# Where the Strassen pairs stand in a down projection: six in place of five in its second half, and the first half's one tile pair later

## The reference

```python
x = x + (jax.nn.silu(u_gate) * u_val) @ w_down[i]     # (256 x 5504) @ (5504 x 2048)
```

## Time and profile before

| | us |
|---|---|
| median of 3 runs | 1431.72 (1431.7 to 1431.96) |
| profiled execution, time | 1431.3 |
| its span, first to last instruction | 1429.5 |

### The profile page before, as it was taken

One profiled execution on the slowest core, in us unless ns is written; L12 is line 12 of the kernel. 1 busy time (PEld: TensorE's weight loads), 2 busy tenths in 40 slices (PEclk: granted clock), 3 DMA queues, 4 the chain that ended last, 5 costly groups with the idle time before them and its releaser, 6 DMA issues.

```text
span 1429.5 us, 19805 instructions
## 1 busy us (share of the span) xinstructions
PE 1419.2 (99%) x7085; PEld 1205.2 (84%) x7085; DVE 1046.8 (73%) x1304; ACT 778.7 (54%) x944; POOL 172.8 (12%) x116
## 2 busy tenths in 40 slices
PE   9999999999999999999999999999999999999997
PEld 7888888888888888888888888888888888888886
DVE  7576777868687865566777767777777988887755
ACT  7555655545454544455555555555555555555644
POOL 0044144110000000000111101111011110000000
PEclk9999999999999999999999999999999999999999
DMA  9655555454655665465656566565665555556653
GB/s 326 197 176 162 162 173 167 149 188 163 222 193 188 220 237 193 155 212 179 193 174 205 178 191 194 173 203 182 191 196 177 205 195 197 171 203 209 232 201 120
DMA packets 190876, 273.47 MB, mean 191 GB/s; under 512 B 11744, under 2 KB 103136, under 8 KB 190688
## 3 DMA queue, kind: packets, MB, share of 16 engines
q1 hardware_dynamic: 190384, 272.30, 58.1%
q10 hardware_dynamic: 432, 0.37, 0.1%
HBM read 270.53 MB, written 2.10 MB: 191 GB/s over the span
## 4 chain that ended last, share of the span: by engine, by line
PE 98%; DVE 1%; issue 0%; DMA 0%; ACT 0%; ACTq 0%; POOLq 0%; POOL 0%; DVEq 0%
PE aux L853 11%; PE main L853 11%; PE main L674 10%; PE main L675 10%; PE main L676 10%; PE aux L862 6%; PE main L862 6%; PE main L732 5%; PE main L733 5%; PE main L734 5%; PE aux L732 3%; PE aux L733 3%; PE aux L734 3%; PE aux L675 2%; PE aux L676 2%; PE aux L674 2%
## 5 line engine op out<-in xcount | busy, mean ns | idle before, releaser
L1439 DVE TENSOR_TENSOR w_lo<-raw,w_hi 128x1024 fp32r<-128x1024 f32 (+1 forms) x481 | 593.0, 1245 | 319.3 <-ACT w_hi L1133 318.6
L1133 ACT ACTIVATE w_hi<-raw 128x1024 fp32r<-128x1024 f32 (+1 forms) x481 | 505.3, 1052 | 502.7 <-PE main L676 155.2
L674 PE MATMUL main<-w_hi,xT 128*128 128x512 f32 x510 | 201.4, 395 | 0.3 <-DVE w_lo L1908 0.3
L675 PE MATMUL main<-w_lo,xT 128*128 128x512 f32 x510 | 198.6, 389 | 0.0
L676 PE MATMUL main<-w_hi,xT 128*128 128x512 f32 x510 | 198.5, 389 | 0.0
L853 PE MATMUL aux<-xT,w_hi 128*128 128x512 f32 x704 | 169.8, 391 | 0.0
L853 PE MATMUL main<-xT,w_hi 128*128 128x512 f32 x672 | 163.0, 391 | 0.0
L853 PEld LDWEIGHTS aux<-xT,w_hi 128*128 128x128 f32 x704 | 129.3, 188 | 25.3 <-issue 0.3
L853 PEld LDWEIGHTS main<-xT,w_hi 128*128 128x128 f32 x672 | 123.2, 188 | 23.6
L2033 POOL TENSOR_TENSOR act<-cv 128x512 f32<-128x512 f32 (+1 forms) x22 | 71.9, 3268 | 418.8 <-DVE cv L1663 418.8
L674 PEld LDWEIGHTS main<-w_hi,xT 128*128 128x128 f32 x510 | 95.8, 188 | 20.0 <-DVE xT L1466 1.0
(11 more groups left out here) (319 smaller groups left out, 2159.3 us busy)
## 6 DMA issues: line engine op xcount, KB each, us to landing
raw<-in_w_up SPq DMA_DIRECT2D x336, 256.0 KB
raw<-in_w_in SPq DMA_DIRECT2D x136, 512.0 KB
raw<-in_w_down SPq DMA_DIRECT2D x84, 512.0 KB
raw<-in_w_out SPq DMA_DIRECT2D x32, 512.0 KB
raw<-in_w_ple_gate SPq DMA_DIRECT2D x32, 512.0 KB
raw<-in_w_branch_a SPq DMA_DIRECT2D x16, 512.0 KB
raw<-in_w_branch_b SPq DMA_DIRECT2D x16, 512.0 KB
raw<-in_w_in SPq DMA_DIRECT2D x15, 256.0 KB, 5.8
```

Source lines behind the costliest of these rows:

```text
L674: pe.matmul(acc, th, wh, start=first, stop=False)
L675: pe.matmul(acc, th, wl, start=False, stop=False)
L1133: ac.activation(w_hi[:, u % RING, :, 0:w], raw[:, u % RING, :, 0:w], ACT.Copy).then_inc(hi_full, 1)
L1439: dve.tensor_tensor(w_lo[:, u % RING, :, 0:w], raw[:, u % RING, :, 0:w], w_hi[:, u % RING, :, 0:w].bitcast(F32), ALU.subtract).then_inc(lo ...
```

## The change

One line: where the Strassen pairs stand.

```diff
-SEVEN_AT = ((5, 8, 11, 14, 17), (5, 8, 11, 14, 17))
+SEVEN_AT = ((6, 9, 12, 15, 18), (4, 7, 10, 12, 15, 17))
```

## The result

The changed kernel takes 1435.66 us (median of 10 runs, 1435.07 to 1436.11) against 1431.71 in the same comparison: a ratio of 1.0026, 95% interval 1.0018 to 1.0035. The prediction was 1435.0, range 1432.4 to 1436.6. The profiled execution took 1435.64, its span is 1433.8 and its granted clock 0.999.

The account below looks back on a forecast made before the run. PE, busy 98%, was taken to bound the kernel, with DVE nearly the bound in the down projection. PE waits of 4.4 plus 0.4 between the pairs, minus 0.68, 0.55 and 0.25, gave +3.3 us: 1435.0, range 1432.4 to 1436.6.

Parts of the forecast that it names:

- One Strassen pair more: Down projection, PE: one more pair of units takes 21 matmuls in place of 24, minus 0.68 us.
- First pair later: First pair of chunks one tile pair later: PE's waits for activation sums and a weight's low part go, minus 0.55 and 0.25.
- Turn: Between the pairs of chunks: ACT's copy waits for later products, delaying DVE's additions; PE loses 0.4 us, bounds 0 and 0.8.
- In hand at the second pair's first: DVE's lead over PE at the second pair's first Strassen pair: 0.3 us, 0.15 after hand-over, bounds 0 and 1.23.
- Rounds: Second pair, L1688 to next L1688: 15.97 us at distance 3, 12.5 and 11.4 at distance 2; 4.4 of PE waits.
- DVE did not catch up at the turn: Rival, between the pairs: DVE catches up, 1.23 in hand, one join in idle time; +0.8 us, 1432.5, chance 0.20.
- the loads did not land sooner: Rival, loads between L1688 and ACT's split: short rounds' loads land sooner; -1.1 us, 1430.6, chance 0.06.
- All of it worse: Rival, down projection: 0.44 lost a round, nothing in hand, 0.8 between the pairs, 0.5 wait kept; +5.1, 1436.8, chance 0.12.

Follow-up runs that it names:

- the version with one short distance: Changed kernel with second pair at 4, 7, 10, 13, 16, 18, GpSimd's join behind the weight sums, its small activation sums later: 1431.51 us, 1.0000 to before.
- half loads: Changed kernel, but each load of the second pair of chunks brings one row tile of two, 256 KB: 1432.23 us, 1.0005 to before.
- half join: Changed kernel, but the second pair's GpSimd joins, from the second on, add one row tile of two: 1432.39 us, 1.0005 to before.
- later join: Changed kernel, but GpSimd's join waits until the weight sums of the Strassen pair before have ended: 1431.47 us, 1.0000 to before.

## Why the prediction was right

Forecast +3.3 from the rows, measured +3.95 in the medians and +3.8 in the stage. Rows of the changed kernel for steps 2 and 3, PE at units 32 and 38, ACT's copy and DVE's fifth addition:

```profile
1173.25 0.39 PE L734 MATMUL main<-w_hi,a_sums_lo 128*128 128x512 f32 x1
1173.71 0.47 PE L732 MATMUL main<-w_hi,aT_hi 128*128 128x512 f32 x1
...
1189.25 0.39 PE L734 MATMUL main<-w_hi,a_sums_lo 128*128 128x512 f32 x1
1189.82 0.47 PE L732 MATMUL main<-w_hi,aT_hi 128*128 128x512 f32 x1 [0.18 <-DVE w_lo L1439]
```

```profile
1198.27 0.60 ACT L1326 ACTIVATE w_sums<-aux 128x512 f32<-128x512 f32 x1 [2.87 <-PE main L734]
```

```profile
1205.65 0.68 DVE L1756 TENSOR_TENSOR w_sums<-aux,w_sums 128x512 f32<-128x512 f32 x1
```

By its steps:

1. **One Strassen pair more, -0.68.** As said. The stage of the version with one short distance, where PE waits for almost nothing, is 1.28 shorter than before: 0.68 and the two waits of the earlier trace rows (0.8), less the turn's 0.3, make 1.2.

2. **First pair later: -0.55 and -0.25.** The first is right: PE has no gap at the first Strassen pair, and the split behind the first sums is 1.37 ahead of PE. The second is not. PE waits 0.24 at unit 32 and 0.34 at unit 38, 0.8 with restarts, where I took none. The mis-sized term is the round: 16.17, 15.99, 16.22 and 16.10, mean 16.12, so 0.48 lost a round and not 0.32; what was in hand went 1.37, 0.84, 0.49 and was gone at the fourth. I had named this end (0.44 a round, 0.5 stays) and not taken it. In the four other runs that leave the first pair and its joins as in the change, the gaps and restarts here come to 0.3 to 0.6, so the 0.8 is that of one execution.

3. **Turn, +0.4.** 0.17 and a restart of 0.14. The copy starts at 1198.27 behind PE, [2.87 <-PE main L734], 4.6 later than in the earlier trace rows, and the fifth addition ends at 1206.33, 0.06 ahead of PE's start. With the first pair left as it was the turn has no gap, so it is the later last Strassen pair that makes it.

4. **In hand at the second pair's first, 0.3.** It was 0.70, hand-over included: the turn had eaten half of the 1.38, not all.

5. **Rounds.** Long ones 16.01, 16.10 and 15.94 for 15.96; short ones 12.70 and 11.41 for 12.5 and 11.4; the load 4.36 in the short round, so nothing lands sooner there, as taken. The half split takes 1.78 because the join falls beside it, as forecast. The second pair's waits with restarts are 4.3 for 4.4: the 0.4 more in hand at the start went into long rounds that were up to 0.14, and a short one that was 0.2, longer. That the total agrees to 0.1 is luck: these are two misses of about 0.4 that cancel.

So the second pair's waits stood in the rows of before, in their cause and, with that luck, in their total. Their places are only partly as forecast: without restarts nothing is lost behind tile pair 7, 0.73 behind 10, 1.63 behind 12, 0.72 behind 15 and 0.33 behind 17, where I had 0.1 to 0.3 behind 7 and 10, about 2 behind 12 and about 1 behind 17. The 0.5 that is missing from the sum in the stage is the first pair's 0.8, less the 0.2 by which the turn and the second pair came out better, to within 0.1. Of the rivals, DVE did not catch up at the turn (0.70 in hand, not 1.23, and no join of the short rounds fell into idle time), and the loads did not land sooner. The half loads show how far this rival's mechanism is right: with loads shorter by 1.5 the second pair's waits are 1.5 us and not 4.3, since the long rounds fall under 15.64. For the short rounds it is wrong: it takes the load's saving off them whole, which would give 11.0 and 9.9, and they came out at 13.37 and 11.42. The prediction calls the load the largest piece of the round and overlooks that DVE's own work, 11.66 and 10.57, is longer than PE's 10.20 by itself. "All of it worse" was right in one of its parts, the first pair's.

## What to carry to other kernels

Where one engine is at 98% and another feeds it in rounds, compare the round, release to release, with the fed engine's work for the same piece. While the round is shorter, an edit that lengthens it is free; once it is longer, each tenth comes out of what is in hand, and then out of the time. Half a microsecond a round decided some 3 us here. An added piece of work that saves 0.68 cost far more than it saved, because it made two rounds in which PE has 10.20 us of work and VectorE, which feeds it, 11.66 and 10.57. So compare the feeding engine's own busy time with the fed engine's work too: where it is longer, no faster load helps in that round, only what was gained in others. Look first for what lies in the round and needn't: moving one GpSimd instruction behind the release was worth as much as the whole change had lost.

## What the runs showed of the hardware

A VectorE instruction of the kind shown here (TENSOR_TENSOR, both inputs in SBUF) that starts during GpSimd's join stands until shortly before the join's row ends, and then takes its plain time. In the changed kernel the half split that starts at 1270.71 stands until 1271.80 (1.09 over its 0.69), and the join's row ends at 1271.95. With the half join the rows above give 1257.58 and 1257.71, with the later join 1259.67 and 1259.81. So what is lost is what is left of the join when the VectorE instruction starts, less 0.13 to 0.15: 1.1, 0.55 and 0.68 us in these three.

The join stands in the same way. It shows 1.30 where VectorE is idle at its start (1258.51, join later). At 1269.74 in the changed kernel an L1713 that runs until 1270.80 was there first, and the join's row is 2.21 long. So a long GpSimd row can be one that was held itself. The Trainium skill's page "SBUF — State Buffer" (SBUF: two separate sides) says that of two such instructions the one that starts first has the pair of ports which the engines share for the whole instruction, and the other blocks fully. The trace agrees, in both directions.

A load of 512 KB takes 4.1 to 4.4 us from release to use in the changed kernel's second pair, at either distance, and one of 256 KB 2.7: 1.5 us for 256 KB more, with two more loads issued on the same queue within 1.1 us in both cases.
